# Gathering the next expert group's tokens beside the last down products, from tokens split once

## The reference, cut to what matters

```python
def routed_moe(x, router_w, router_b, w_gate, w_up, w_down):
    B, S, D = x.shape
    xt = x.reshape(B * S, D)
    aff = jax.nn.sigmoid((xt @ router_w).astype(jnp.float32))
    sel = aff + router_b.astype(jnp.float32)
    grp_score = lax.top_k(sel.reshape(-1, N_GROUPS, EXPERTS_PER_GROUP), 2)[0].sum(-1)
    _, g_idx = lax.top_k(grp_score, TOPK_GROUPS)
    ...
    gates = jnp.einsum('nk,nke->ne', w, jax.nn.one_hot(e_idx, N_EXPERTS, dtype=jnp.float32)).astype(x.dtype)
    y = jnp.zeros_like(xt)
    for e in range(N_EXPERTS):
        h = jax.nn.silu(xt @ w_gate[e]) * (xt @ w_up[e])
        y = y + gates[:, e:e + 1] * (h @ w_down[e])
    return y.reshape(B, S, D)

def second_block(x, ...):
    for l in range(DEPTH):
        ...
        x = layer_norm_2(ALPHA * x + mix, ln_g[l, 0], ln_b[l, 0])
        ffn = routed_moe(x, router_w, router_b, moe_w_gate[l], moe_w_up[l], moe_w_down[l])
        x = layer_norm_2(ALPHA * x + ffn, ln_g[l, 1], ln_b[l, 1])
    return x
```

## Time and profile before

| | before |
|---|---|
| median of 3 runs | 2546.51 us (2530.24 to 2579.36) |
| profiled execution | 2524.17 us, of which its span is 2522.4 us |
| PE busy | 2392.1 us, 95% of the span |
| DVE, ACT busy | 68%, 47% |
| DMA | 501.19 MB, mean 199 GB/s |
| chain that ended last | PE 69%, DVE 17%, ACT 9% |

### The profile page before, as it was taken

How to read it: one execution, slowest core, us unless ns; L and a number is a source line. 1 busy time by engine, 2 the same in 40 slices (tenths; PEclk the granted TensorE clock), 3 DMA queues, 4 the chain that set the end, 5 groups by cost and what they waited for, 6 DMA issues and landing times.

```text
span 2522.4 us, 34116 instructions
## 1 busy us (share of the span) xinstructions
PE 2392.1 (95%) x14290; PEld 2056.2 (82%) x14290; DVE 1719.7 (68%) x2274; ACT 1191.6 (47%) x1525; POOL 98.7 (4%) x187
## 2 busy tenths in 40 slices
PE   7999999898989999999999999989999899899997
PEld 3778888767789999998999997867787787678776
DVE  5997777743676656655666654567878776688776
ACT  3212212334544444445544443456766654566665
POOL 0111111010000000000000000000000000000000
PEclk9999999999999999999999999999999999999999
DMA  7777877322124554455444543337977621388774
GB/s 278 229 236 263 270 261 259 134 91 100 67 78 165 177 196 160 180 191 219 150 151 176 192 168 109 104 143 295 351 293 291 245 111 65 147 317 336 282 294 174
DMA packets 80387, 501.19 MB, mean 199 GB/s; under 512 B 9604, under 2 KB 10708, under 8 KB 28496
## 3 DMA queue, kind: packets, MB, share of 16 engines
q1 hardware_dynamic: 59120, 423.66, 45.2%
q0 software_dynamic: 21088, 75.01, 9.3%
HBM read 497.58 MB, written 1.05 MB: 198 GB/s over the span
## 4 chain that ended last, share of the span: by engine, by line
PE 69%; DVE 17%; ACT 9%; issue 3%; DMA 1%; ACTq 0%; DVEq 0%; SPq 0%
PE bank L406 67%; DVE wl L1984 8%; ACT wh L1363 6%; DVE macc L2020 1%; ACT s L1461 1%; DVE f L2179 1%; PE bank L630 1%; DVE s L2170 1%; DVE rs L2044 1%; DMA raw<-in_wmod 1%; PE bank L1257 1%; DMA mring<-in_wmod 0%; DVE hl L2154 0%; ACT H L1470 0%; DVE tmpm L2147 0%
## 5 line engine op out<-in xcount | busy, mean ns | idle before, releaser
L1984 DVE TENSOR_TENSOR wl<-raw,wh 128x2048 fp32r<-128x2048 f32 (+1 forms) x432 | 904.0, 2098 | 403.3 <-ACT wh L1363 399.7
L1363 ACT ACTIVATE wh<-raw 128x2048 fp32r<-128x2048 f32 (+1 forms) x432 | 755.3, 1756 | 360.4 <-PE bank L406 358.0
L406 PE MATMUL bank<-hh,wh 128*128 128x258 f32 (+2 forms) x2200 | 692.0, 315 | 32.7 <-DVE wl L1984 7.7
L406 PE MATMUL bank<-hh,wl 128*128 128x258 f32 (+2 forms) x2200 | 673.5, 306 | 0.0
L406 PE MATMUL bank<-hl,wh 128*128 128x258 f32 (+2 forms) x2200 | 671.9, 305 | 0.0
L406 PEld LDWEIGHTS bank<-hh,wh 128*128 128x128 f32 x2200 | 420.4, 191 | 61.8 <-DVE wl L1984 8.0
L406 PEld LDWEIGHTS bank<-hl,wh 128*128 128x128 f32 x2200 | 421.1, 191 | 18.5
L406 PEld LDWEIGHTS bank<-hh,wl 128*128 128x128 f32 x2200 | 419.1, 191 | 19.0
L406 PE MATMUL bank<-wh,hh 128*128 128x512 f32 (+1 forms) x704 | 278.3, 395 | 5.4 <-DVE hl L2932 2.8
L406 PE MATMUL bank<-wh,hl 128*128 128x512 f32 (+1 forms) x704 | 273.9, 389 | 0.0
L406 PE MATMUL bank<-wl,hh 128*128 128x512 f32 (+1 forms) x704 | 273.8, 389 | 0.0
(11 more groups left out here) (444 smaller groups left out, 2644.1 us busy)
## 6 DMA issues: line engine op xcount, KB each, us to landing
raw<-in_wstream SPq DMA_DIRECT2D x393, 1024.0 KB, 4.9
mring<-in_wmod POOLq DMA_DIRECT2D x128, 512.0 KB, 4.6
raw<-in_wmod SPq DMA_DIRECT2D x6, 1024.0 KB, 6.5
X<-in_xT SPq DMA_DIRECT2D x1, 2048.0 KB, 12.1
mods<-in_wmod SPq DMA_DIRECT2D x2, 1024.0 KB, 18.5
bias<-in_nabias POOLq DMA_DIRECT2D x16, 128.0 KB, 2.5
c_sglg<-in_sglg POOLq DMA_DIRECT2D x1, 1024.0 KB, 4.9
c_sglb<-in_sglb POOLq DMA_DIRECT2D x1, 1024.0 KB, 6.9
```

What stands on the lines that cost most here:

```text
L406: return e.matmul(out, lhsT, rhs, start=start, stop=stop, skip_group_check=True)
L1363: e.activation(wh[i % NB][:, o], raw[i % NR][:, o], ACT.Copy).then_inc(*slab_high(st.split + m))
L1984: e.tensor_tensor(wl[i % NB][:, o], raw[i % NR][:, o], wh[i % NB][:, o].bitcast(F32), ALU.subtract).then_inc(*slab_low(st.split + m))
```

## The change

The tokens are split once per layer: `Xt` holds the high part (fp32r, still copied by ACT), and a new tile `Xl` the low part, which DVE computes in four subtractions of 128 x 512, placed behind the gates and ahead of `rank`, `flag` and `Pm`. `Pm` becomes fp32r. A block of the gather is now four fp32r matmuls of 256 columns, high part in the first half of a bank and low part in the second; ACT copies the one half to `hh`, DVE the other to `hl`, always all 256 columns. Banks are 0 and 1 in turn. The gather of group 0 stands ahead of the flag's load. That of group g+1 stands in group g: blocks 0, 1 behind `turn_h(3)`, blocks 2, 3 ahead of `down(3, 0)`, blocks 4, 5 ahead of `down(3, 1)`, blocks 6, 7 behind it and ahead of `pt`. ACT and DVE have the same places, between their weight splits.

```diff
--- before.py
+++ after.py
@@ -306,8 +306,9 @@
             q.iota = const(ph, f"iota{l}", [P, T], dram["iota"].partition_broadcast(P))
             q.rank = sb(ph, f"rank{l}", [P, 2, 4])
             q.flag = sb(ph, f"flag{l}", [1, 4], I32)
-            q.Pm = sb(ph, f"Pm{l}", [P, 4, 2, T])
-            q.Xt = sb(ph, f"Xt{l}", [P, 2, D])
+            q.Pm = sb(ph, f"Pm{l}", [P, 4, 2, T], F32R)
+            q.Xt = sb(ph, f"XtH{l}", [P, 2, D], F32R)
+            q.Xl = sb(ph, f"XtL{l}", [P, 2, D], F32R)
             q.YH = sb(ph, f"YH{l}", [P, 2, D], F32R)
             q.YL = sb(ph, f"YL{l}", [P, 2, D], F32R)
             q.PT = sb(ph, f"PT{l}", [P, 2 * T], F32R)
@@ -1179,7 +1180,7 @@
             ins.then_inc(*result("aff t", l))
             for s_ in range(2):
                 for half in range(2):
-                    b = bank(("xt", l, s_, half), act_out, "xt", l, s_, half)
+                    b = bank(("xt", l, s_, half), dve_out, "xt l", l, s_, half)
                     for d in range(4):
                         ins = e.transpose(b[:, P * d:P * d + P], X[:, 4 * half + d, P * s_:P * s_ + P], ident[:])
                     ins.then_inc(*result("xt", l, s_, half))
@@ -1207,26 +1208,25 @@
                     if after is not None and d >= 2:
                         after(d - 2)
 
+
+            def gather(g, ds):
+                w.wait_ge(dve_out, "xt l", l, 1, 1)
+                w.wait_ge(dve_out, "pm", l, g)
+                for d in ds:
+                    b = claim(d % 2, ("xe", l, g, d), dve_out, "xe l", l, g, d)
+                    for i, x in enumerate((q.Xt, q.Xl)):
+                        for s_ in range(2):
+                            ins = mm(b[:, T * i:T * i + T], x[:, s_, P * d:P * d + P], q.Pm[:, g, s_, :], i == 0 and s_ == 0, s_ == 1)
+                    ins.then_inc(*result("xe", l, g, d))
+
             def group(g, n):
                 S = n // P
                 blocks = [(s_, slice(P * s_, P * s_ + P)) for s_ in range(S)]
-                turn = [0]
-
-                def small(key, by, *drained):
-                    turn[0] += 1
-                    return claim(turn[0] % 4, key, by, *drained)
-
-                w.wait_ge(act_out, "xt", l, 1, 1)
-                w.wait_ge(dve_out, "pm", l, g)
-                for d in range(KC):
-                    b = small(("xe", l, g, d), dve_out, "xe l", l, g, d)
-                    for s_ in range(2):
-                        ins = mm(b[:, 0:n], q.Xt[:, s_, P * d:P * d + P], q.Pm[:, g, s_, 0:n], s_ == 0, s_ == 1)
-                    ins.then_inc(*result("xe", l, g, d))
-                b = small(("ge", l, g), dve_out, "ge", l, g)
+
+                b = claim(3, ("ge", l, g), dve_out, "ge", l, g)
                 for s_, c in blocks:
                     for t in range(2):
-                        ins = mm(b[:, 4 * s_:4 * s_ + 4], q.Pm[:, g, t, c], q.R[5][:, t, 4 * g:4 * g + 4], t == 0, t == 1)
+                        ins = mm(b[:, 4 * s_:4 * s_ + 4], q.Pm[:, g, t, c].bitcast(F32), q.R[5][:, t, 4 * g:4 * g + 4], t == 0, t == 1)
                 ins.then_inc(*result("ge", l, g))
 
                 def product(x, o, bs, *key):
@@ -1278,29 +1278,39 @@
                 turn_h(0)
                 up(1)
                 for x in range(1, 4):
+                    if x == 3:
+                        result.mark("h read", "moe", l, g)
                     down(x - 1, 0)
                     turn_h(x)
+                    if x == 3 and g < 3:
+                        gather(g + 1, (0, 1))
                     down(x - 1, 1)
                     if x < 3:
                         gate(x + 1)
                         up(x + 1)
-                result.mark("h read", "moe", l, g)
-                down(3, 0)
-                down(3, 1)
+                for part in range(2):
+                    if g < 3:
+                        gather(g + 1, (2 + 2 * part, 3 + 2 * part))
+                    down(3, part)
+                if g < 3:
+                    gather(g + 1, (6, 7))
                 claim(0, ("pt", l, g), act_out, "PT", l, g)
                 for s_ in range(2):
                     for t in range(2):
                         ins = e.transpose(banks[0][:, T * s_ + P * t:T * s_ + P * t + P],
-                                          q.Pm[:, g, t, P * s_:P * s_ + P], ident[:])
+                                          q.Pm[:, g, t, P * s_:P * s_ + P].bitcast(F32), ident[:])
                 ins.then_inc(*result("pt", l, g))
                 for b in range(8):
-                    if b < 2:
+                    if b == 0 or b == 1 and g == 3:
                         st.drain[b] = (act_out, "PT", l, g)
+                    elif b == 1:
+                        st.drain[b] = (dve_out, "xe l", l, g + 1, 7)
                     elif b < 4:
                         st.drain[b] = (dve_out, "HL", l, g, 3)
                     else:
                         st.drain[b] = (dve_out, "YL", l, g, b % 2)
 
+            gather(0, range(KC))
             w.wait_ge(dve_out, "flag", l)
             for g in range(4):
                 was = (result.count, dict(w.heard), dict(st.drain), st.tile, len(order))
@@ -1877,6 +1887,14 @@
                     e.activation(q.Xt[:, s_, 512 * half:512 * half + 512], banks[bank_of["xt", l, s_, half]][:],
                                  ACT.Copy).then_inc(*act_out("xt", l, s_, half))
 
+            def gather(g, ds):
+                w.wait_ge(result, "h read", *(("moe", l, g - 1) if g else ("wo0", "wo1")[l:l + 1]))
+                for d in ds:
+                    w.wait_ge(result, "xe", l, g, d)
+                    e.activation(hh[:, d, 0:T], banks[bank_of["xe", l, g, d]][:, 0:T], ACT.Copy).then_inc(*act_out("xe", l, g, d))
+
+            gather(0, range(KC))
+
             def group(g, n):
                 S = n // P
                 blocks = [(s_, s_ == S - 1, slice(P * s_, P * s_ + P)) for s_ in range(S)]
@@ -1884,11 +1902,6 @@
                 def ended(ins, last, *key):
                     if last:
                         ins.then_inc(*act_out(*key))
-
-                w.wait_ge(result, "h read", *(("moe", l, g - 1) if g else ("wo0", "wo1")[l:l + 1]))
-                for d in range(KC):
-                    w.wait_ge(result, "xe", l, g, d)
-                    e.activation(hh[:, d, 0:n], banks[bank_of["xe", l, g, d]][:, 0:n], ACT.Copy).then_inc(*act_out("xe", l, g, d))
 
                 def gate(x):
                     taken(4 * KC)
@@ -1915,16 +1928,24 @@
                 for x in range(1, 4):
                     taken(2 * KC)
                     turn_h(x)
+                    if x == 3 and g < 3:
+                        gather(g + 1, (0, 1))
                     taken(2 * KC)
                     if x < 3:
                         gate(x + 1)
                         taken(4 * KC)
-                taken(4 * KC)
+                for part in range(2):
+                    if g < 3:
+                        gather(g + 1, (2 + 2 * part, 3 + 2 * part))
+                    taken(2 * KC)
+                if g < 3:
+                    gather(g + 1, (6, 7))
                 w.wait_ge(result, "pt", l, g)
                 if g:
                     w.wait_ge(result, "scat", l, g - 1, KC - 1)
                 e.activation(q.PT[:], banks[0][:], ACT.Copy).then_inc(*act_out("PT", l, g))
                 w.wait_ge(result, "down", l, g, 3)
+                w.wait_ge(pool_out, "zero", l)
                 for half in range(2):
                     o = slice(512 * half, 512 * half + 512)
                     for s_, last, _ in blocks:
@@ -2898,6 +2919,12 @@
             step(e.reciprocal(q.sm[:, 3, :], q.sm[:, 2, :]), "1/weight")
             behind()
             e.tensor_tensor(gt[:], gt[:], q.sm[:, 3, :].unsqueeze(2).to_broadcast([P, 2, 16]), ALU.mult).then_inc(*dve_out("gates", l))
+            for s_ in range(2):
+                for half in range(2):
+                    c = slice(512 * half, 512 * half + 512)
+                    w.wait_ge(act_out, "xt", l, s_, half)
+                    e.tensor_tensor(q.Xl[:, s_, c], banks[bank_of["xt", l, s_, half]][:], q.Xt[:, s_, c].bitcast(F32),
+                                    ALU.subtract).then_inc(*dve_out("xt l", l, s_, half))
             b = banks[bank_of["rank", l]]
             w.wait_ge(result, "rank", l)
             behind()
@@ -2919,6 +2946,13 @@
                     e.scalar_tensor_tensor(X[:, d, 0:T], X[:, d, 0:T], ALPHA if g == 0 else 1.0, banks[b0 + d % 2][:, 0:T], ALU.mult,
                                            ALU.add).then_inc(*dve_out("moe x", l, g, d))
 
+            def gather(g, ds):
+                for d in ds:
+                    w.wait_ge(act_out, "xe", l, g, d)
+                    e.tensor_copy(hl[:, d, 0:T], banks[bank_of["xe", l, g, d]][:, T:2 * T]).then_inc(*dve_out("xe l", l, g, d))
+
+            gather(0, range(KC))
+
             def group(g, n):
                 S = n // P
```

(4 more changed lines are left out.)

## The result

The changed kernel takes 2592.04 us (median of 6 runs, 2584.48 to 2620.80), the kernel before 2551.69 us (6 runs, 2530.24 to 2579.36). The ratio is 1.0195, with a 95% interval from 1.0153 to 1.0237: the change costs 50 us (39 to 60), about 2%, where 19 us were forecast, and the time lies at the upper end of the stated range (2538 to 2592). Ratios here are taken over the fast executions of each kernel and medians over all of them, so the two can differ: the two medians above lie 40 us apart.

A forecast was written before the change was run, and what follows sets the result against it. PE bounds the kernel between boundaries, full at 2.4 GHz. Boundaries +4.7, clock +8 and layer starts +6.4 sum to 19 us; on 2546.5 that gives 2565.5, say 2565, range 2538 to 2592.

The forecast's parts named there:

- What is the pause?: PE's idle behind the `pt` transposes: loading the flag and jumping over the body of 256, 1.76 to 2.38 us.
- pause 2.0: Between the `pt` transposes and the `ge` matmuls at a group's end: PE idle for 2.0 us.
- the boundary: From one group of experts to the next: 8.6 us with blocks 0 to 5, six 51.6 against 46.9, +4.7 us.
- Nothing that PE could run hides the pause: At a group's end: the gather now ahead of the jump was behind it before, not beside it; pause 2.0 us.
- The clock: At the six group boundaries: PE falls to 1.2 GHz at nearly each, 1.3 us apiece, +8 us.
- The start of a layer: Subtractions ahead of `rank`, gather in two banks, uncovered flag and branch: +3.2 us a layer, +6.4 for two.
- The pause is a wait: Rival, behind the transposes: a wait and not the jump; boundary 6.75 us, time about 2548; chance 0.13.
- Faster: Rival, inside groups: down products leave PE room, blocks 0 to 5 cost nothing; -5.7 us, 2541; chance 0.07.
- The clock did not stay full: Judges the rival that PE's clock stays full at the boundaries: +11 us, 2557.5; chance 0.20.
- the weights were in time: Judges the rival of weight splits queuing behind waits for PE's gather: 55 us, 2601; chance 0.05.

## Why the prediction was wrong

- **What held.** PE was full inside the groups and each pair of blocks cost 0.93 us there, 2.8 in six blocks, as forecast. DVE's split stood ahead of block 6 and the transposes started 2.3 us behind the down products (2.65 forecast). A gather's work on PE was unchanged. The clock fell at the boundaries. No weight came late: within the two stages PE waits for no `wl`.
- **The step that failed** is "What is the pause?", and with it the term "pause 2.0" of the boundary. I named the jump rightly, but took the 1.76 to 2.38 us of the earlier trace rows for its whole length. They were the part that stuck out, and "Nothing that PE could run hides the pause" was the wrong sentence: the last down product had hidden most of it. The jump runs from the moment when PE's instruction stream has no unmet wait ahead of it. In the kernel before that was the split of the last half product's slab. Here is its trace at the second boundary:

```profile
1819.04 4.66 DVE L1984 TENSOR_TENSOR wl<-raw,wh 128x2048 fp32r<-128x2048 f32 x2 [0.67 <-ACT wh L1363]
...
1824.80 0.60 PE L1293 MATMUL bank<-c_ident,Pm 128*128 128x128 f32 x4
...
1827.27 3.83 PE L406 MATMUL bank<-Pm,Xt 128*128 128x128 f32 x32 [1.88 <-ACT YH L1931]
```

- The first of the two splits ends at about 1821.3, 3.5 us ahead of the transposes, and the gather begins 5.9 us later: two thirds of the jump had lain beside the last down product and the transposes. That this split is the last unmet wait is worked out from the order of the code and its time; that such a wait decides is what the added and the removed wait show. The changed kernel took that cover away. I had seen that the transposes would wait for DVE, and counted the wait (1.7 us), but not that the jump queues behind it. The six pauses are 40.3 us (9.05 + 6.25 + 6.34 + 6.18 + 6.17 + 6.34) where 12 were forecast. These 28 us are nearly all of the 31 by which the forecast of 19 fell short of 50; the clock cost 4 more than its 8, and the starts of the layers 2 less.
- **The clock** was forecast at +8. The stages grew by 49.5 us, of which the boundaries and the inner blocks are 63.3 + 16.8 - 46.9 = 33.2 and the starts of the layers 4; the remaining 12 us is the half clock of the gate products behind the pauses. Of the granted clock the same comes out: from a gate to the next transposes it averages 0.96 to 0.98 in the six groups behind a pause, where it was 1.00 before, and that is 13 us lost. The mechanism was right, the size too small; the pauses were longer than forecast. The Trainium skill says (TensorE: Matmul & The Clock Gate, "HAM oscillation") that idle gaps between bursts of matmuls bring the slow clock back each time. The windows at the first boundary agree, 0.50 in the pause and behind it.
- **The start of a layer** was forecast at +3.2 each and measured at 2.2 and 2.5: the gather starts 0.3 to 0.4 later against `rank`'s matmuls, and the gate 1.9 to 2.1 later against the gather. The flag and the branch take little there; the rows around the branch:

```profile
1684.40 0.39 PE L407 MATMUL bank<-Pm,XtL 128*128 128x256 f32 x2
1685.08 0.60 PE L407 MATMUL bank<-R,Pm 128*128 128x4 f32 x4 [0.28 <-issue]
1685.53 0.48 PE L407 MATMUL bank<-wh,hh 128*128 128x512 f32 x1
```

- That is 0.28 us idle where 1.0 was taken: no body is jumped over there, that of 128 follows at once.
- **The rivals.** "The pause is a wait" is out: `YH` is copied by 1945.0 at the third boundary, and PE starts at 1949.73. "Faster" is out for this change. The clock did not stay full, and the weights were in time. What did come was a rival that I had not written down: a cover that the kernel before had on its instruction stream, taken away by a wait.

## What to carry to other kernels

A wait ahead of a far jump costs its own length and, on top, as much of the jump as earlier work would have covered; before placing one there, look for the last wait that is still unmet when the engine's instructions get to it, and move such waits (or the jump) so that as much queued work lies behind them as the jump takes, here some 7 us. A pause that a profile shows is what sticks out, not the length of what causes it, and it bounds that length from below only. Where spans of whole executions differ by the clock of stages that nobody touched, compare the stage.

## What the hardware showed that I had not expected

- A jump over about 600 rows of matmuls costs PE 6.5 to 7.1 us from the last unmet wait in the kernels with `ge` first behind it, and 5.2 to 5.9 us at the second boundary in those with the gather first behind it (one wait added, and the kernel before). Why these two differ was not tried. DVE, whose groups have some 50 rows in the trace where PE's have 376, passes the same boundary in well under 1 us (`hl` followed `YL` by 0.43 us at the third boundary before), but stood for 4.58 us when it had four bodies to jump over.
- The first boundary of the first layer takes longer than the others: the jump 9.8 to 10.5 us instead of 7 with `ge` first behind it (pauses of 9.05 against 6.2; 7.08 against 4.3; 4.39 against 0.8), and 0.4 to 0.9 us more with the gather first. The first boundary of the second layer does not. No experiment looks at why; it stays open.
- PE can run for tens of us at half clock while it is busy. In the kernel before with one branch, in a stage of small matmuls that the edit doesn't touch:

```profile
2090.00:2150.00 60.00, 60.00 (x200) 43.58 (x199) 26.68 (x79) 16.65 (x56) 0.00 (x0) 0.50 0.05 18
```

- The kernel before was at the full clock in the same stage. At half clock for 60 us, that is about 30 us of this execution, as much as most effects in this study. It differs from one profiled execution to the other, and I take it for the main part of the spread of the 25 runs of the kernel before (2527 to 2575 us, and 2521 to 2579); only profiled executions show it. The intervals of 10 runs reach about 10 us to each side, so times alone don't tell kernels apart that differ by 8 us.
